# Two transformer blocks in one kernel on one core: the second block's mixer in another order, two norms taken in one pass, and shorter start and norm chains

## What is computed

```
x  = rms_norm(h, norm_final_g)                      # h: the first block's output
xn = rms_norm(x, norm1_g_2)
proj = xn @ w_in_2 + b_in_2                         # conv a | conv gate | q | k | v
c = a * sigmoid(gate)                               # 1024 channels
c = silu(layer_norm(causal_conv_31_taps(c) + b))    # per channel over time
o = window_attention(rotary(rms_norm(q)), rotary(rms_norm(k)), v)
x = x + concat(c, o) @ w_out_2
x = x + peer(rms_norm(x, norm2_g_2))                # product-key experts, 16384 of them
```

## Time and profile before

| | us |
|---|---|
| median of 3 runs | 3468.71 (3468.04 to 3469.47) |
| the profiled execution | 3467.83 |
| its span, first to last instruction | 3466.0 |
| PE busy in the span | 3322.4 (96%) |
| DVE busy | 2176.4 (63%) |
| ACT busy | 1603.1 (46%) |

### The profile page before, as it was taken

The page is one execution under the profiler, slowest core; times in us unless marked ns, Lnnn a source line. Parts: engine busy times, 40 slices in busy tenths (PEclk is TensorE's granted clock), DMA queues, the critical chain, the costliest instruction groups (busy, mean ns, idle before and its releaser), DMA issues.

```text
span 3466.0 us, 54836 instructions
## 1 busy us (share of the span) xinstructions
PE 3322.4 (96%) x22090; PEld 2930.5 (85%) x22090; DVE 2176.4 (63%) x2946; ACT 1603.1 (46%) x2110; POOL 3.5 (0%) x10
## 2 busy tenths in 40 slices
PE   7999999999999999887979999899999999999999
PEld 6999998788888887776869989888888888888887
DVE  5664455666576565676358998558666566755554
ACT  4554444455455454445554444443444444435353
POOL 0000000000000000000000000000000000000000
PEclk9999999999999999988999999999999999999999
DMA  6445555555555555431244454454555555555554
GB/s 218 167 148 188 207 184 176 187 190 194 189 185 192 183 194 177 136 128 67 91 146 158 162 173 144 149 183 145 183 170 176 185 183 176 172 180 185 194 186 166
DMA packets 161115, 590.63 MB, mean 170 GB/s; under 512 B 17888, under 2 KB 17920, under 8 KB 159584
## 3 DMA queue, kind: packets, MB, share of 16 engines
q1 hardware_dynamic: 160624, 586.69, 50.0%
q0 software_dynamic: 240, 0.44, 0.1%
HBM read 584.96 MB, written 2.10 MB: 169 GB/s over the span
## 4 chain that ended last, share of the span: by engine, by line
PE 88%; DVE 9%; ACT 2%; issue 1%; DMA 0%; DVEq 0%; SPq 0%; ACTq 0%
PE PS L405 18%; PE PS L363 12%; PE PS L365 12%; PE PS L364 12%; PE PS L406 9%; PE PS L373 6%; PE PS L374 6%; PE PS L375 6%; DVE LO L289 2%; PE PS L1214 2%; PE PS L958 2%; DVE GB L929 1%; PE PS L624 0%; DMA GB<-in_norms 0%; ACT HI L288 0%
## 5 line engine op out<-in xcount | busy, mean ns | idle before, releaser
L289 DVE TENSOR_TENSOR LO<-RAW,HI 128x1024 fp32r<-128x1024 f32 (+1 forms) x1096 | 1329.5, 1219 | 928.6 <-ACT HI L288 924.8
L288 ACT ACTIVATE HI<-RAW 128x1024 fp32r<-128x1024 f32 (+1 forms) x1096 | 1150.7, 1054 | 1186.4 <-PE PS L365 604.6
L405 PE MATMUL PS<-XX,HI 128*128 128x512 f32 x2688 | 949.4, 398 | 0.0
L406 PE MATMUL PS<-XX,LO 128*128 128x256 f32 x2688 | 754.3, 281 | 0.0
L373 PE MATMUL PS<-XX,HI 128*128 128x256 f32 x2176 | 626.3, 288 | 31.7 <-DVE LO L289 27.9
L363 PE MATMUL PS<-HI,FH 128*128 128x512 f32 x1504 | 595.8, 396 | 23.8 <-DVE FL L501 18.8
L374 PE MATMUL PS<-XX,HI 128*128 128x256 f32 x2176 | 618.2, 284 | 0.0
L375 PE MATMUL PS<-XX,LO 128*128 128x256 f32 x2176 | 617.8, 284 | 0.0
L405 PEld LDWEIGHTS PS<-XX,HI 128*128 128x128 f32 x2688 | 504.6, 188 | 121.7
L365 PE MATMUL PS<-HI,FL 128*128 128x512 f32 x1504 | 588.4, 391 | 0.0
L364 PE MATMUL PS<-LO,FH 128*128 128x512 f32 x1504 | 587.5, 391 | 0.0
(11 more groups left out here) (236 smaller groups left out, 2355.5 us busy)
## 6 DMA issues: line engine op xcount, KB each, us to landing
RAW<-in_peer_v SPq DMA_DIRECT2D x256, 512.0 KB, 3.3
RAW<-in_ffn_w_up SPq DMA_DIRECT2D x176, 512.0 KB, 4.2
RAW<-in_peer_ut_rest SPq DMA_DIRECT2D x160, 512.0 KB, 3.3
RAW<-in_w_in SPq DMA_DIRECT2D x136, 512.0 KB, 4.1
RAW<-in_peer_ut SPq DMA_DIRECT2D x96, 512.0 KB, 3.3
RAW<-in_ffn_w_down SPq DMA_DIRECT2D x88, 512.0 KB, 4.3
RAW<-in_w_mix_out SPq DMA_DIRECT2D x32, 512.0 KB, 4.2
RAW<-in_w_in_2c SPq DMA_DIRECT2D x32, 512.0 KB, 3.3
```

What stands on the lines that cost most here:

```text
L288: hi_done.append(AC.do(lambda e, raw=raw, hi=hi: e.activation(hi, raw, ACT.Copy), landed[i], used))
L289: lo_done.append(DV.do(lambda e, raw=raw, hi=hi, lo=lo: e.tensor_tensor(lo, raw, hi.bitcast(F32), ALU.subtract), hi_done[i], landed[i], used))
L405: e.matmul(o, hi[:, k, w], x, start=u == 0 and k == 0, stop=False, skip_group_check=True)
L406: m = e.matmul(o[:, 0:S], lo[:, k, w], x[:, 0:S], start=False, stop=u == 3 and k == 3, skip_group_check=True)
```

## The change

In the diff's order, with the names it uses:

- **Start.** Only the identity matrix of the constants is fetched ahead of the first norm weight, on SP; the rest of the constants and the parameters wait on POOL until that weight has landed, and so do POOL's small loads behind them.
- **`product_both`** runs its four 512-column matmuls first and then its four 256-column ones.
- **`rstd`** has two fused DVE operations in place of four plain ones, so three DVE operations are left behind the Sqrt, with the last. `root_table()` runs a Sqrt on a constant ahead of the squares of each norm.
- **The two norms between the blocks** become one pass: `residual_both` sums the squares of RES and of RES times the first weight while the last feed-forward products run, `scale_of_both` makes both scales from them, GB1 is multiplied by GB beforehand, and RES is scaled only behind `normed`.
- **The second mixer** runs: convolution input for channels 0 to 3, q, k and v, convolution input for channels 4 to 7. Channels 0 to 3 are convolved on DVE with three taps for each unit, starting behind the first pair; the norm of the heads is cut into pieces that run as `background` beside the second pair, the attention behind it. The loop then holds the rest of the attention, channel 4 on DVE, and channels 5 to 7 on PE, one after another.
- **The layer norm** becomes a generator of pieces that runs as `background` beside the output product's attention half. The weight of the last norm, the keys and the q/k/v bias are fetched by POOL.

```diff
+    m_ident = SP.dma(lambda e: e.dma_start(CONST[:, 0:128], a["consts"][:, 0:128]), l_ident)
     m_gb = SP.dma(lambda e: e.dma_start(GB[:], rows(a["norms"][0])), l_gb)
-    m_par = PO.dma(lambda e: e.dma_start(PAR[:], a["params"]), l_par)
+    m_const = PO.dma(lambda e: e.dma_start(CONST[:, 128:N_CONST], a["consts"][:, 128:N_CONST]), l_const, m_gb)
+    m_par = PO.dma(lambda e: e.dma_start(PAR[:], a["params"]), l_par, m_gb)
...
+    add_units("w_in_2c", [2, 0])
     add_units("w_in_2q", [0, 1])
     add_units("w_in_2kv", [0], 256)
-    add_units("w_in_2c", [2, 0, 3, 1])
+    add_units("w_in_2c", [3, 1])
...
-                        x = XX[:, 4 * u + k, :, :].rearrange("p h s -> p (h s)")
-                        e.matmul(o, hi[:, k, w], x, start=u == 0 and k == 0, stop=False, skip_group_check=True)
-                        m = e.matmul(o[:, 0:S], lo[:, k, w], x[:, 0:S], start=False, stop=u == 3 and k == 3,
+                        e.matmul(o, hi[:, k, w], XX[:, 4 * u + k, :, :].rearrange("p h s -> p (h s)"),
+                                 start=u == 0 and k == 0, stop=False, skip_group_check=True)
+                    for k in range(4):
+                        m = e.matmul(o[:, 0:S], lo[:, k, w], XH[:, 4 * u + k, :], start=False, stop=u == 3 and k == 3,
                                      skip_group_check=True)
...
-        m4 = DV.do(lambda e: e.tensor_tensor(ss, y, y, ALU.mult), m3)
-        m5 = DV.do(lambda e: e.tensor_tensor(ss, ss, v, ALU.mult), m4)
-        m6 = DV.do(lambda e: e.tensor_scalar(ss, ss, -0.5, 1.5, ALU.mult, ALU.add), m5)
-        return DV.do(lambda e: e.tensor_tensor(y, y, ss, ALU.mult), m6)
+        m3 = DV.do(lambda e: e.tensor_tensor(ss, y, y, ALU.mult), m2)
+        m4 = DV.do(lambda e: e.scalar_tensor_tensor(out=ss, in0=ss, scalar=-0.5, in1=v, op0=ALU.mult, op1=ALU.mult),
+                   m3)
+        return DV.do(lambda e: e.scalar_tensor_tensor(out=y, in0=ss, scalar=1.5, in1=y, op0=ALU.add, op1=ALU.mult),
+                     m4)
...
+    def root_table():
+        roots[0] = AC.do(lambda e: e.activation(SM[:, 25:26], SM[:, 24:25], ACT.Sqrt), m_one, roots[0])
+    def scale_of_both(m):
+        ss, v, y1, y2, y = (SM[:, 232 + at:232 + at + n] for at, n in ((0, 4), (4, 2), (6, 2), (8, 2), (10, 2)))
+        parts = SM[:, 0:32].rearrange("p (k x) -> p k x", k=2)[:, :, 0:8].rearrange("p k (t g) -> p k t g", t=2)
+        m = DV.do(lambda e: e.tensor_reduce(ss.rearrange("p (k t) -> p k t", k=2), parts, AX.X, ALU.add), m)
+        m1 = m = rstd(ss[:, 0:2], 1.0 / D, v, y1, m)
+        for _ in range(2):
+            m = DV.do(lambda e: e.tensor_tensor(ss[:, 2:4], ss[:, 2:4], y1, ALU.mult), m)
+        m = rstd(ss[:, 2:4], 1.0 / D, v, y2, m)
+        return y1, m1, (y, DV.do(lambda e: e.tensor_tensor(y, y1, y2, ALU.mult), m))
...
+    def residual_both(banks, m, g, *more):
+        c = slice(512 * g, 512 * g + 512)
+        if g == 3:
+            root_table()
+        marks = residual(banks, m, g, False, *more)
+        for t in range(2):
+            m_junk[t] = squares(RES[:, t, c], t, g, JUNK[:, t, :], marks[t], ff_free, m_junk[t])
+        for t in range(2):
+            r = DV.do(lambda e, t=t: e.tensor_tensor(UN[:, t, c], RES[:, t, c], GB[:, c], ALU.mult), marks[t], m_gb,
+                      un_free)
+            squares(UN[:, t, c], t, g, UN[:, t, c], r, into=SSG)
+        return marks
...
-    y1, m = scale_of(4, m_ssq[0])
+    y1, m_y1, both = scale_of_both(m_ssq[0])
+    x_ready, m_un, m_un_read = normed(both, GB1, m_gb1, m_x_read)
     for q in range(4):
         for t in range(2):
-            m_res = scaled(RES, y1, GB, q, t, m, m_gb)
-            squares(RES[:, t, 512 * q:512 * q + 512], t, q, UN[:, t, 512 * q:512 * q + 512], m_res)
-    m_bi = SP.dma(lambda e: e.dma_start(GB[:, 0:1280], rows(a["b_qkv_2"])), l_gb, m_res)
-    x_ready, m_un, m_un_read = normed(4, GB1, m_gb1, m_x_read)
+            m_res = scaled(RES, y1, GB, q, t, m_y1, m_gb)
+    BI = UF[:].rearrange("p c s -> p (c s)")[:, 0:1280]
+    m_bi = PO.dma(lambda e: e.dma_start(BI, rows(a["b_qkv_2"])), l_bi, m_down)
...
+    m_h = conv_input(0, None)
+    beside.append(causal([0, 1, 2, 3], m_h, 3))
...
+    background.append(together(heads_normed(0), heads_normed(1)))
+    background.append(attention(2, Z2[:, :, 0:1024], KD2, V2, QT2, KT2, sc2, PT2, const("mask2"), SINK[:, 1, :], 8,
+                                m_qk, box2, False))
+    m_h = conv_input(1, m_h)
     m_x_read = mm_done[-1]
+    beside.append(causal([4], m_h, 3))
+    on_pe = [causal_pe(c, m_h) for c in (5, 6, 7)]
+    rate[0] = 2
     while on_pe or 1 not in box2:
         step()
         advance(on_pe)
+    while beside:
+        advance(beside)
...
+    background.append(layer_normed())
     for g in range(4):
         pair, banks, m = product(True, 8, FH, FL, lambda k: [box2[0], box2[1]], k0=8)
         acc_free[pair] = residual(banks, m, g, False, m_res)
     flush()
```

More of the change, by code:

```diff
@@ L213, in _program @@
     l_xt = [landing(f"l_x{t}") for t in range(2)]
-    l_const, l_par, l_small, l_gb, l_gb1, l_keys, l_out = [landing("l_" + n) for n in
-                                                      ("const", "par", "small", "gb", "gb1", "keys", "out")]
+    l_ident, l_const, l_par, l_small, l_gb, l_gb1, l_bi, l_gb2, l_keys, l_out = [landing("l_" + n) for n in (
+        "ident", "const", "par", "small", "gb", "gb1", "bi", "gb2", "keys", "out")]
     l_raw = [landing(f"l_raw{i}") for i in range(NRAW)]
@@ L767, in residual @@
         marks = []
+        if last and g == 3:
+            root_table()
         for t in range(2):
@@ new lines, in _program @@
+    m_h = conv_input(0, None)
+    beside.append(causal([0, 1, 2, 3], m_h, 3))
+    z_done = [[], []]
+    for g in range(3):
+        w = 512 if g < 2 else 256
+        pair, banks, m = product(True, 16, XH, XL, x_ready, width=w)
+        free = []
+        for t in range(2):
+            d = Z2[:, t, 512 * g:512 * g + w]
+            r = DV.do(lambda e, d=d, g=g, w=w, b=banks[t]: e.tensor_tensor(
+                d, b[:, 0:w], BI[:, 512 * g:512 * g + w], ALU.add), m, m_bi, arena_free)
+            free.append(r)
+            z_done[t].append(r)
+        acc_free[pair] = free
@@ L986, in _program, with layer_normed, summed @@
     rate[0] = 1
+    conv_ready = []
+    def layer_normed():
+        nonlocal m_gb, m_keys
+        i, b, fr = spare()
+        held.add(i)
+        mu = b[:, 0:S]
+        HV = HP[:].rearrange("p c s -> p (c s)")[:, 0:2048].rearrange("p (c s) -> p c s", c=8)
+        def summed(o, src, c, m):
+            return PE.do(lambda e: e.matmul(o, const("mean"), src[:, c, :], start=c == 0, stop=c == 7,
+                                            skip_group_check=True), m)
+        for c in range(8):
+            m = summed(mu, CV, c, [fr, m_cv[c]])
+            if c == 3:
+                yield
+        yield
+        i2, b, fr = spare()
+        held.add(i2)
+        var = b[:, 0:S]
+        quarters, m_sq = [], []
+        for q in range(4):
+            c2 = slice(2 * q, 2 * q + 2)
+            quarters.append(DV.do(lambda e, c2=c2: e.tensor_tensor(
+                CV[:, c2, :], CV[:, c2, :], mu.unsqueeze(1).to_broadcast([128, 2, S]), ALU.subtract), m))
+            m_sq.append(AC.do(lambda e, c2=c2: e.activation(HV[:, c2, :], CV[:, c2, :], ACT.Square), quarters[q],
+                              m_cv))
+            if q % 2:
+                yield
+        t_free[i] = quarters
+        held.discard(i)
+        for q in range(4):
+            for c in (2 * q, 2 * q + 1):
+                m = summed(var, HV, c, [fr, m_sq[q]])
+            if q == 1:
+                yield
+        yield
+        vv, yy = SG[:, 0, :], SG[:, 1, :]
+        t_free[i2] = m = DV.do(lambda e: e.tensor_copy(SG[:, 2, :], var), m)
+        held.discard(i2)
+        m_yy = rstd(SG[:, 2, :], 1.0, vv, yy, m)
+        yield
+        for half in range(2):
+            c4 = slice(4 * half, 4 * half + 4)
+            m = DV.do(lambda e, c4=c4: e.tensor_tensor(CV[:, c4, :], CV[:, c4, :], yy.unsqueeze(1).to_broadcast(
+                [128, 4, S]), ALU.mult), m_yy)
+            ms = [AC.do(lambda e, c=c: e.activation(HV[:, c, :], CV[:, c, :], ACT.Silu, bias=par("lnb", c),
+                                                    scale=par("lng", c)), m)
+                  for c in range(4 * half, 4 * half + 4)]
+            yield
+            conv_ready.append(split(FH[:, 4 * half:4 * half + 4, :], FL[:, 4 * half:4 * half + 4, :],
+                                    HV[:, 4 * half:4 * half + 4, :], ms, m_down, dg_read, m_bi_read))
+            yield
+        m_gb = PO.dma(lambda e: e.dma_start(GB[:], rows(a["norms"][4])), l_gb2, ms)
+        m_keys = PO.dma(lambda e: e.dma_start(KEYT[:], a["keys"]), l_keys, box2["pt_read"], ms)
@@ L987, in _program @@
+    m_keys = None
+    background.append(layer_normed())
     for g in range(4):
```

177 lines of the change are left out of this document (68 added, 109 removed).

## The result

The changed kernel takes 3427.69 us (median of 4 runs, 3424.86 to 3428.12); beside it on the same chip the kernel before took 3469.09 us (3468.04 to 3470.02). The ratio is 0.9878, 95% interval 0.9864 to 0.9892: 41.4 us faster. The prediction was 3427, in a range from 3396 to 3455. The profiled execution took 3428.12 us, with a span of 3426.3 and a granted clock of 0.986.

The account below looks back on a forecast made before the run. PE, busy 96% of the span, was taken as the bound, so savings must come from its stalls, clock or pace. Terms 5.5 + 1.7 + 19.7 + 14.2 = 41.1 us off 3467.8 gave 3427, range 3396 to 3455.

Parts of the forecast that it names:

- Start: First norm: scaling no longer waits for GB behind other transfers; 5.5 us saved, bounds 1.8 and 6.
- Table and `rstd`: Feed-forward and last norms: no table wait before the Sqrt and one DVE operation fewer; 2 x 0.9 = 1.7 us saved.
- `product_both`: Its 2688 matmul pairs: taking turns costs nothing, so grouping gives 0, within 1 us.
- the sum of the two: In `product_both`, a pair in turn takes 346.7 ns, the sum of uniform spacings 120.0 and 226.7 ns.
- Two norms in one: Between the blocks: 5.4 us less, but 4 come back as a stall in the first product; bounds 0 to 5.4.
- The mixer's stages: Second mixer: first product 15.3, first convolution input 50.1, DVE-paced q/k/v and second input 117, loop 103; 285.4 us together.
- the sum of its phases: Mixer's loop: ACT's phases 48, PE's 42 and DVE's 13 us follow one another; 103 us.
- the mixer's 19.7: Second mixer: its stages take 285.4 us instead of 305.1; 19.7 saved.
- the change of order gives nothing: Rival, mixer: the lone convolution's saving returns in DVE's 117 and a loop of about 123 us; 3447, within a 0.16 case.
- The rival of half speed in all of PE's own phases: Mixer's loop: PE's phases all at 1.2 GHz add 42 us; 3469, no change; chance of 3462 to 3475: 0.05.
- Layer norm: Beside the output product: 12.1 us of waiting goes and full clock gives 2.1 more; 14.2 saved.
- Slower: Rival, loop: convolution doesn't fill attention's waits; loop 172 us, kernel 3496, deciding from a loop of 152; chance 0.06.

Follow-up runs that it names:

- x_order: Changed kernel with only the matmul order in `product_both` put back to 512 and 256 columns in turn: 3431.13 us, ratio 0.9897 to the kernel before.
- x_norms: Changed kernel with the two norms between the blocks put back one behind the other: 3424.29 us, ratio 0.9866 to the kernel before.
- x_rot: Changed kernel with the rotary angles' VectorE chain issued in the feed-forward stage and the stream's eight scalings beside the mixer's first products: 3421.41 us.
- x_diag: Changed kernel with the 93 diagonal matrices of the convolution on TensorE built on VectorE instead of ScalarE: 3412.68 us.
- x_seq: Changed kernel with q, k and v first again, then both convolution inputs, heads' norm and attention in the background behind q, k and v: 3417.50 us.

## Why the prediction was right, and where its steps were not

The time was right to a us, and of its five terms the start, the tables and the layer norm came out near their size. That it was right to a us is partly luck: the mixer gave 3.0 us less than forecast, and `product_both` 2.5 that were not forecast. The reasons inside the largest term, the mixer, were not all right.

- **Start**, 5.5 forecast: 5.08 in the trace, 4.2 by taking it back. Table and `rstd` at the two norms: 1.7 forecast, 1.4 measured (from the last matmul before the norm to the first behind it 12.88 to 12.41 and 12.88 to 12.00). Table loads again showed no drain: the first one took 1.28 us from 0.73, with the Sqrt 0.02 behind it, at 2.03. So the longer price in the Trainium skill (ScalarE: Activation LUTs, What ACT_TABLE_LOAD costs) is again not seen in this kernel's traces.
- **`product_both`**, 0 within 1 us: a mis-sized term, -2.5 from before to after and -3.5 for the order alone (x_order). The failed step is that the spacing of the first third was taken for all 2688 pairs; a second sample anywhere later would have shown 353 ns instead of 347. That a pair in turn was "the sum of the two" uniform spacings was no argument either: in groups the 512-column matmuls take 232.5 ns, not 226.7.
- **Two norms in one**: 15.3 forecast to the first product, 15.05 measured, and a stall of 4 forecast, 3.77 measured. What was left out is the half clock behind that stall, 2.8 us more in this trace, which turns the part into a loss (x_norms) until the work ahead of LO is moved (x_rot).
- **The mixer's stages**: 15.3 + 50.1 + 117 + 103 = 285.4 forecast; 15.0 + 52.9 + 119.6 + 100.6 = 288.1 measured. The stage of q, k, v and the second input was put down to VectorE throughout. It is PE's in q/k/v (55.15 of 55.20). In the second input PE lost 9.7 of 64.4 us, 5.7 in four waits for LO and 4.0 in one for the heads' norm (L545 for KD), all of them on VectorE, which is busy 58.21. So the 117 came near 119.6 by a path half of which was another engine's. The loop was 2.4 us shorter than the sum of its phases, and the sum holds: the exponentials and scalings last 44 us in ACT's two phases, forecast as 48, and taking diagonals off them shortens the loop (x_diag).
- **What the order is worth**: the step that failed is to credit the mixer's 19.7 to the new order. x_seq, with the old order and all else of the change, is 10.8 us shorter than after up to the expert part, so the new order took 10.8 away, in the loop because attention starts later. All else together would then have given 27.5 where 16.7 was measured; how much of that is due to the pieces beside the products, no run takes apart. The rival "the change of order gives nothing" saw the mechanism too mildly and put it in the wrong place: VectorE's stage rather than attention's start.
- **Clock**: the loop ran at 0.86, and 0.88 to 0.92 in its variants. The rival of half speed in all of PE's own phases did not happen: in PE's phases, 1605.0 to 1625.0 and 1649.8 to 1665.6, the clock was 1.00 and 0.99, and the lower means, 0.88 and 0.73, are ACT's phases. By the rule of the Trainium skill (TensorE: Matmul & The Clock Gate, HAM oscillation) each burst would pay again; here the fall shows behind waits, as at 1404, but these two bursts of 20.0 and 15.8 us ran at full clock.
- **Layer norm**: 14.2 forecast, 13.7 in the trace, 13.9 by taking it back.
- **Slower**: a loop of 152 us would have been needed; it was 100.6.

## What to carry to other kernels

A time that comes out right does not show that the reasons are: of this change's two headline parts, the order of the mixer and the merged norm, each was a loss where it stood, and the gain came from the rest of the change: what was laid beside the products, the layer norm and the start. When a stage is reordered, ask first which chain of dependent steps will now start later (here the softmax of the first query tile), and only then which engine has room. When work is moved off one path, look at what the engine that gets it has queued next, and price a stop of PE above its length: here 3.75 to 4.2 us cost 5.2 to 7.9, with the half clock behind them.

## What the runs showed of the hardware that was not expected

- Matmuls of 512 and 256 columns with a weight load each: in turn, a pair took 346.5 to 346.7 ns in one stage and 353.3 in every other, in both kernels that take turns; in groups of four it took 350.8 everywhere. The cause was not found.
- A stop of 3.77 us cost 6.6 us in one trace, since the granted clock stood at 1.2 GHz for some 7 us behind it (window clock 0.94, against 1.00 without the stop). A stop of 3.75 us at the same place in x_diag had 3.4 us at 1.2 GHz behind it and cost 5.2 (window clock 0.97).
- POOL's queue of tiny pieces: the DMA dip of the earlier trace rows vanished when they and the large tables were put behind GB, with the rate at 381 to 444 GB/s from 3 to 19 us, and came back (74 to 161 GB/s from 8 to 11 us) when both were put back.
